# A hybrid decoder layer with mixture of experts: bias columns instead of bias products in the wide jobs, and folds moved to GpSimd

## The reference

```
hid = jnp.dot(xblk, w1[e]) + b1[e]            # 1024 -> 2048
glu = jnp.minimum(hid[:, 0::2], 7.0)
lin = jnp.clip(hid[:, 1::2], -7.0, 7.0)
act = glu * jax.nn.sigmoid(1.702 * glu) * (lin + 1.0)
yb  = jnp.dot(act, w2[e]) + b2[e]             # 1024 -> 1024, then times the gate
```

## Time and profile before

| | |
|---|---|
| median of three runs | 2207.58 us |
| the profiled execution | 2204.4 us |
| its span | 2202.7 us |
| TensorE (PE) busy | 2060.5 us, 94% |
| VectorE (DVE) busy | 1600.2 us, 73% |
| ScalarE (ACT) busy | 1294.2 us, 59% |
| GpSimd (POOL) busy | 420.0 us, 19% |
| mean granted TensorE clock | 0.973 |

### The profile page before, as it was taken

The page is one execution under the profiler, slowest core; times in us unless marked ns, Lnnn a source line. Parts: engine busy times, 40 slices in busy tenths (PEclk is TensorE's granted clock), DMA queues, the critical chain, the costliest instruction groups (busy, mean ns, idle before and its releaser), DMA issues. The chain is left out here.

```text
span 2202.7 us, 40551 instructions
## 1 busy us (share of the span) xinstructions
PE 2060.5 (94%) x11750; PEld 1774.1 (81%) x11751; DVE 1600.2 (73%) x2206; ACT 1294.2 (59%) x1867; POOL 420.0 (19%) x478
## 2 busy tenths in 40 slices
PE   7999978778967999999999999999999999999994
PEld 6888867777856888889798897889898888979883
DVE  5342166985657687978878787788788797887876
ACT  5221245563436576766757677677667676675765
POOL 3100000220231121211213122122212131121311
PEclk9999979999978999999999999999999999999997
DMA  5221120004346897979889798899798897988978
GB/s 182 61 82 54 43 96 1 11 20 140 106 163 241 284 314 242 353 250 329 290 269 332 240 351 267 296 313 358 254 318 299 259 348 250 332 284 276 332 240 309
DMA packets 260787, 506.10 MB, mean 230 GB/s; under 512 B 34369, under 2 KB 35394, under 8 KB 260440
## 3 DMA queue, kind: packets, MB, share of 16 engines
q1 hardware_dynamic: 242938, 458.05, 60.3%
q0 software_dynamic: 17792, 47.33, 8.8%
q10 hardware_dynamic: 4, 0.02, 0.0%
HBM read 466.10 MB, written 39.22 MB: 229 GB/s over the span
## 5 line engine op out<-in xcount | busy, mean ns | idle before, releaser
L1819 DVE TENSOR_TENSOR wlo<-raw,whi 128x1024 fp32r<-128x1024 f32 x774 | 931.3, 1218 | 72.2 <-ACT whi L1295 53.1
L1295 ACT ACTIVATE whi<-raw 128x1024 fp32r<-128x1024 f32 x775 | 845.3, 1116 | 216.4 <-PE ps L984 161.1
L982 PE MATMUL ps<-xT,whi 128*128 128x320 f32 x1920 | 524.8, 349 | 6.2 <-DMA brow<-brow_d 6.2
L984 PE MATMUL ps<-xT,wlo 128*128 128x160 f32 x1920 | 455.6, 237 | 0.0
L982 PEld LDWEIGHTS ps<-xT,whi 128*128 128x128 f32 x1920 | 363.5, 189 | 10.7 <-issue 6.0
L984 PEld LDWEIGHTS ps<-xT,wlo 128*128 128x128 f32 x1920 | 369.0, 192 | 0.2
L2087 POOL DMA_INDIRECT acc_d<-y,icur x64 | 102.7, 1604 | 943.2 <-ACT y L1329 880.6
L619 PE MATMUL ps<-whi,xT 128*128 128x512 f32 x544 | 215.8, 397 | 0.0
L619 PE MATMUL ps<-whi,aT 128*128 128x512 f32 x512 | 212.9, 416 | 1.3
L621 PE MATMUL ps<-whi,xT 128*128 128x512 f32 x544 | 213.0, 392 | 0.0
L620 PE MATMUL ps<-wlo,xT 128*128 128x512 f32 x544 | 212.8, 391 | 0.0
(11 more groups left out here) (299 smaller groups left out, 3540.4 us busy)
## 6 DMA issues: line engine op xcount, KB each, us to landing
raw<-in_w SPq DMA_DIRECT2D x780, 512.0 KB
raw<-in_w_in SPq DMA_DIRECT2D x16, 512.0 KB
xs<-in_x SPq DMA_DIRECT2D x8, 512.0 KB, 7.1
raw<-in_w_out SPq DMA_DIRECT2D x8, 512.0 KB
mix<-in_x SPq DMA_DIRECT2D x8, 512.0 KB, 4.1
acc_d<-mix SPq DMA_DIRECT2D x8, 512.0 KB
h_d<-h SPq DMA_DIRECT2D x8, 512.0 KB
mix<-acc_d SPq DMA_DIRECT2D x8, 512.0 KB, 7.7
```

The costliest lines, as they stand in the source:

```text
L982: pe.matmul(o2, wh[:, a, cols], xT2[:, :, k, 0:JOB_T], start=q == 0 and a == 0, stop=False, skip_group_check=True)
L984: m = pe.matmul(o, wl[:, a, cols], xT2[:, 0, k, 0:JOB_T], start=False, stop=q == QUARTERS - 1 and a == 1, skip_group_check=True)
L1295: act.activation(parted(slot(whis, s)), paired(raw_slot(s), s), ACT.Copy).then_inc(split_hi, 1)
L1819: dve.tensor_tensor(parted(slot(wlos, s)), paired(raw_slot(s), s), parted(slot(whis, s).bitcast(F32)), ALU.subtract).then_inc(split_lo, 1)
```

## The change

The b1 biases of the wide jobs leave TensorE's chains. In the front, TensorE transposes the raw biases of the 32 experts (gate and linear ones apart) into bank 1, VectorE copies them out (and adds 1 to the linear ones), SP writes them to DRAM and reads them back later, as columns, into a place that is free then. Before each job GpSimd copies the job's 2 x 8 columns into `bcur`. In a wide job ScalarE adds the gate bias as the activation's bias, in two activations instead of one, and VectorE adds the linear bias to `lsum` by one more operation. The fold of the 32 further rows is now done by GpSimd from SBUF: ScalarE evacuates both blocks (64 partitions) into `y`, GpSimd copies the lower block to `yfold` and adds it to the upper one. TensorE, ScalarE, VectorE, SP and GpSimd get the waits that go with it.

```diff
 # TensorE, between the halves of unit 0
+            def bias_turn():
+                pe.wait_ge(bias_in, 16 * 5)
+                pe.wait_ge(turned_lo, FIRST_FREE)
+                for two in range(2):
+                    for i in range(BTILES):
+                        cols = slice(2 * P * i + two, 2 * P * (i + 1) + two - 1, 2)
+                        m = pe.transpose(ps[:, 1, (two * BTILES + i) * NE:(two * BTILES + i + 1) * NE],
+                                         bp[0:NE, cols], ident[0:NE, 0:NE])
+                m.then_inc(bias_turned, 1)
+            bias_turn()
 # first_unit
+                if half == 1 and q == 0:
+                    pe.wait_ge(bturn_set, 1)
 # wide_step
-                        if q == 0:
-                            pe.matmul(o, brow[:, c * UNIT + 256 * odd + P * i:c * UNIT + 256 * odd + P * (i + 1)], ones2[:, 0:JOB_T],
-                                      start=False, stop=False, skip_group_check=True)
 # SP, before the wait for bias_hi; and before the router weights
+            sp.wait_ge(bturn_set, 1)
+            sp.dma_start(bcolT_d, bturn[:, :, :, :]).then_inc(bturn_out, 16)
...
+            sp.wait_ge(bturn_out, 16)
+            sp.dma_start(bcolT[:, :, :, :], bcolT_d).then_inc(bcolT_in, 16)
 # ScalarE: unit 0's chains; wide activation; block 1
+                        act.wait_ge(bturn_out, 16)
...
-                    act.activation(sigw[:, :, :], gsum[:, :, :], ACT.Gelu_apprx_sigmoid).then_inc(sig_set, 1)
+                    if c == 0:
+                        act.wait_ge(bcur_set, j + 1)
+                    for i in range(2):
+                        m = act.activation(sigw[:, i, :], gsum[:, i, :], ACT.Gelu_apprx_sigmoid,
+                                           bias=bcur[:, 0, 2 * c + i:2 * c + i + 1])
+                    m.then_inc(sig_set, 1)
...
-                    act.wait_ge(y_set[1], j * 2 + c - 3)
-                    act.activation(yfold[:, c - 4, :], ps[HALF:2 * HALF, out_bank(2, c, 1), :], ACT.Copy,
-                                   scale=gcur[HALF:2 * HALF, 1:2]).then_inc(yfolded, 1)
+                    act.activation(y[0:2 * HALF, 1, (c - 4) * UNIT:(c - 3) * UNIT], ps[0:2 * HALF, out_bank(2, c, 1), :], ACT.Copy,
+                                   scale=gcur[0:2 * HALF, 1:2]).then_inc(yfolded, 1)
 # VectorE: behind the lower bounds; the linear bias; y_fold and its calls are gone
+            dve.wait_ge(bias_turned, 1)
+            dve.tensor_copy(bturn[:, 0, :, :], ps[:, 1, 0:BTILES * NE].rearrange("p (i e) -> p i e", e=NE))
+            dve.tensor_scalar(bturn[:, 1, :, :], ps[:, 1, BTILES * NE:2 * BTILES * NE].rearrange("p (i e) -> p i e", e=NE),
+                              1.0, None, ALU.add).then_inc(bturn_set, 1)
...
+                dve.tensor_tensor(lsum[:, :, :], lsum[:, :, :],
+                                  bcur[:, 1, 2 * c:2 * c + 2].unsqueeze(2).broadcast_to([P, 2, JOB_T]),
+                                  ALU.add).then_inc(lin_biased, 1)
+                dve.wait_ge(lin_biased, j * 4 + c + 1)
 # GpSimd
+            def columns(e):
+                pool.tensor_copy(bcur[:, :, :], bcolT[:, :, :, e].rearrange("p a i o -> p a (i o)")).then_inc(bcur_set, 1)
+            def next_bias(j, e):
+                wait(act_set, j * 4 + 4)
+                columns(bass.ds(e, 1))
+                wait(bcur_set, j + 2)
+            def y_fold(j, c):
+                wait(yfolded, j * 2 + c - 3)
+                cols = slice((c - 4) * UNIT, (c - 3) * UNIT)
+                pool.tensor_copy(yfold[:, c - 4, :], y[HALF:2 * HALF, 1, cols]).then_inc(low_moved, 1)
+                pool.wait_ge(low_moved, j * 2 + c - 3)
+                pool.tensor_tensor(y[0:HALF, 1, cols], y[0:HALF, 1, cols], yfold[:, c - 4, :], ALU.add).then_inc(y_set[1], 1)
+                pool.wait_ge(y_set[1], j * 2 + c - 1)
 # GpSimd's job: behind load_slots; before the scatters
+                e = pool.value_load(jobt[0:1, 0, bass.ds(j + 1, 1)], min_val=0, max_val=NE - 1)
...
+                if blocks == 2:
+                    next_bias(j, e)
+                    y_fold(j, 4)
+                    y_fold(j, 5)
                 for b in ((0, 1) if blocks == 2 else (1, 0)):
+                    if b == 0 and blocks == 1:
+                        pool.sem_inc(low_moved, 2)
+                        next_bias(j, e)
```

More of the change, by code:

```diff
@@ L81 @@
 B_AV, B_HI, B_HG, B_OUT = 0, 128, 640, 1152
+BTILES = FF // P
 F32 = mybir.dt.float32
@@ L112, in build @@
     brow_d = dram("brow_d", (NE + 1, 2, BW))
+    bcolT_d = dram("bcolT_d", (P, 2, BTILES, NE))
     raw = at("raw", 0, [P, QUARTERS, 2, UNIT])
@@ L150, in build @@
     tinit = at("tinit", B + 68 * KB, [P, PAD_ROWS, 2])
+    bturn = at("bturn", B, [P, 2, BTILES, NE])
     hf = at("hf", B, [P, HH, T])
@@ L180, in build @@
     glw = at("glw", B + 55.75 * KB, [P, 2, 2, JOB_T])
+    bcur = at("bcur", B + 58.25 * KB, [P, 2, BTILES])
     yfold = at("yfold", B + 60 * KB, [HALF, 2, UNIT])
+    bcolT = at("bcolT", B + 64 * KB, [P, 2, BTILES, NE])
     R = [B + 72.5 * KB]
@@ L326, in build @@
         rooted, eps_set, brow_zero = sem("rooted"), sem("eps_set"), sem("brow_zero")
-        lin_set, yfolded = sem("lin_set"), sem("yfolded")
+        lin_set, yfolded, low_moved = sem("lin_set"), sem("yfolded"), sem("low_moved")
+        bias_turned, bturn_set, bturn_out, bcolT_in, bcur_set = (
+            sem(n) for n in ("bias_turned", "bturn_set", "bturn_out", "bcolT_in", "bcur_set"))
+        lin_biased = sem("lin_biased")
         pool_mark, sync_mark, act_mark = sem("pool_mark"), sem("sync_mark"), sem("act_mark")
@@ L342, in build @@
         FIRST = [0, 2, 4, 6, 1, 3, 5, 7]
+        FIRST_FREE = 2 * NT
         def x_bank(i):
@@ L1871, in hidden_wide @@
                 dve.wait_ge(sum_taken, j * 8 + 2 * c + 2)
+                if c == 0:
+                    dve.wait_ge(bcur_set, j + 1)
+                dve.tensor_tensor(lsum[:, :, :], lsum[:, :, :],
+                                  bcur[:, 1, 2 * c:2 * c + 2].unsqueeze(2).broadcast_to([P, 2, JOB_T]),
+                                  ALU.add).then_inc(lin_biased, 1)
+                dve.wait_ge(lin_biased, j * 4 + c + 1)
                 dve.tensor_scalar(lsum[:, :, :], lsum[:, :, :], 1.0 + LIMIT, 1.0 - LIMIT, ALU.min,
@@ L1886, in aT_wide @@
                                   aTh[:, k, 1, 0:HALF].bitcast(F32), ALU.subtract).then_inc(aT_lo, 1)
[L1888 to L1893, removed]
             def job(j, blocks):
@@ L1898, in job @@
                         (hidden if blocks == 1 else hidden_wide)(j, UNIT_END[s - 1])
-                    if blocks == 2 and UNIT_END.get(s - 1, 0) == 4:
-                        y_fold(j, 4)
                     jsplit(j, s + AHEAD)
@@ L1910, in job @@
                 if blocks == 2:
-                    y_fold(j, 5)
                     dve.sem_inc(hid_taken, 4)
@@ L1915, in job @@
                     dve.sem_inc(lin_set, 4)
+                    dve.sem_inc(lin_biased, 4)
             for s in range(4):
@@ L2106, in _ @@
             pool.wait_ge(y_zero, 1)
+            pool.wait_ge(bcolT_in, 16)
+            columns(slice(0, 1))
+            pool.wait_ge(bcur_set, 1)
             with pool.Fori(0, JOBS, 1) as j:
```

## The result

The kernel after has a median of 2219.29 us (2214.33 to 2229.77, nine runs), the kernel before 2209.54 us in the same nine rounds: ratio 1.0062, 95% interval 1.0049 to 1.0074, so slower, by some 14 us by the ratio. The profiled execution took 2224.26 us, with a span of 2222.6; the pair of profiles is 19.9 us apart, about twice the difference of the medians, and terms read from the pair have to be taken so.

A forecast was written before the change was run, and what follows sets the result against it. TensorE's instruction count was taken as the bound, with any transfer or engine late enough to stop it. 2204.4 - 29 + 16.5 + 22 - 2.4 = 2211.5, plus 3.2 for the median: 2215 us; 8-in-10 range 2195 to 2233.

The forecast's parts named there:

- Term 1: Wide jobs: 240 bias products leave TensorE's chains at 0.12 us each, a gain of 29 us.
- Term 2: Front: TensorE waits for VectorE's copies of the turned biases, 13.9 us plus 2.6 for half clock, a loss of 16.5 us.
- Rival 3: Front: VectorE copies before its small operations are through, TensorE hardly waits, some 1.5 us remain; 2200 us, chance 0.07.
- Term 3: Narrow jobs behind wide ones: GpSimd's folds delay scatters and gathers 3.4 us, TensorE stalls, a loss of 22 us.
- Term 4: Job stage: four of TensorE's waits for the bias row go as narrow jobs lengthen, a gain of 2.4 us.
- Rival 1: Narrow jobs: folds delay GpSimd under 1.3 us, gathers stay in time; 2193 us, up to 2203; chance 0.27.
- Rival 2: Nine tight narrow jobs, step 18: pauses of 2.5 us and more bring half clock, 2.6 us each; 2246 us, chance 0.11.
- Rival 4: Narrow jobs: GpSimd's locks starve VectorE and TensorE waits for splits, 1 us in each of 15; 2230 us, chance 0.05.

The follow-up runs named there:

- one memset: Changed kernel with folds back on ScalarE and VectorE, plus one GpSimd clear, waited for, ahead of a wide job's first scatter: 2205.34 us, ratio 0.9998 to the kernel before.

## Why the prediction was right, and where it was wrong

The sum came out: 2215 against 2219.29, slower as said, with 7 us of loss forecast and 14 measured by the ratio. Its steps did not all.

**Term 1, -29: right in kind, a little too large.** A wide job lasts 54.72 us instead of 56.54, 0.11 us for each bias product and 27 us in all. In the kernels without the wait for the row it is 55.0 (the 0.17 us wait for a bank is part of this): there the products are worth 15 x 1.53 = 23 us. The sentence "no product waits for the new additions" holds, but I did not look at what the shorter step runs into next.

**Term 2, +16.5: right.** Pause 12.85 us (49.70 to 62.55) where 13.9 was said, since GpSimd's third subtraction ended sooner than the old small operation suggested; half clock 2.6 us. The scores were 15.6 us late. Rival 3 had the right remedy: with the copies first TensorE hardly waits. The lockout is the rule of the Trainium skill (SBUF — State Buffer, "Who interferes with whom"). The trace agrees for the operations with two SBUF inputs (2.18 to 4.31 us for 4 elements). By the same section a VectorE instruction with at most one SBUF input, outside the modes that use both ports, doesn't contend with GpSimd. The trace agrees for the copies out of PSUM, which took 0.42 and 0.41 us beside GpSimd's subtraction; the operation at L1491, with one input and in SBUF, was held 2.39 us, and no run here shows in which mode it ran.

**Term 3, +22: the amount right, the mechanism wrong.** The folds cost 24 us (1.0114 alone; 1.0062 against 0.9955 in the change). GpSimd's delay was said to be 3.4 us and is 3.1; 1.30 us for the addition and 0.61 and 1.36 for the copies lie inside the bounds. What failed is "what is behind shifts alike. TensorE stalls" at the gathered rows. The first gather was issued only 1.7 us later, since the copy of the gates and the slots' transfer were shorter, and it landed about when it was wanted: 2.3 us of stalls instead of 20. The transfers themselves shifted, and they share 16 engines with the weights. The table by stretch, from the narrow job's start in steps of 2 us, before (last three columns: clock, share of the DMA engines, GB/s):

```profile
968.80:970.80 2.00, 2.00 (x10) 1.63 (x9) 1.29 (x3) 1.89 (x4) 0.06 (x1) 1.00 0.07 27
...
972.80:974.80 2.00, 2.00 (x11) 1.64 (x10) 2.00 (x2) 2.00 (x3) 1.44 (x2) 1.00 1.04 158
974.80:976.80 2.00, 2.00 (x10) 1.65 (x9) 2.00 (x3) 0.28 (x1) 1.44 (x2) 1.00 1.03 188
...
978.80:980.80 2.00, 2.00 (x10) 1.64 (x10) 1.98 (x3) 2.00 (x3) 0.57 (x2) 1.00 0.99 354
...
982.80:984.80 2.00, 2.00 (x12) 1.61 (x11) 1.98 (x4) 1.79 (x3) 0.00 (x0) 1.00 1.06 406
```

and after:

```profile
988.80:990.80 2.00, 2.00 (x11) 1.65 (x10) 1.22 (x2) 2.00 (x2) 1.92 (x2) 1.00 0.42 144
...
992.80:994.80 2.00, 2.00 (x10) 1.65 (x9) 2.00 (x4) 0.30 (x2) 1.70 (x2) 1.00 0.57 148
994.80:996.80 2.00, 2.00 (x10) 1.68 (x9) 1.96 (x3) 2.00 (x3) 1.39 (x3) 1.00 1.02 167
...
998.80:1000.80 2.00, 2.00 (x11) 1.64 (x10) 2.00 (x3) 1.21 (x3) 0.81 (x2) 1.00 1.04 276
```

Before, the scatter's traffic fills the engines from 4 to 8 us behind the start (158 to 188 GB/s), and from 10 us on the loads run at 354. After, the engines are mostly half busy until 8 us, and the scatter falls at 8 to 12 us, when loads have queued. The view of the transfers says whose traffic it is. From 972.8 to 976.8 us, before, GpSimd's queue has 0.57 MB and 94.3% of the engines, and SP's 0.13 MB and 9.5%. From 994.8 to 998.8 us, after, GpSimd's has 0.41 MB and 63.4%, and SP's 0.36 MB and 37.1%. In the first 16 us of the job GpSimd's queue moves 0.66 MB in both kernels and takes no more of the engines after (23.9% against 27.1%), but SP's moves 2.85 MB instead of 3.17. What is lost is the idle time ahead of the scatter. From there the engines are full to the end of the job (share 1.05), so the loads never make it up and the last of the queue, the row, has it all. These 0.32 MB are 0.8 us at 390 GB/s, and TensorE waits 1.82 us for this row; where the rest arises is not shown. I had read the row's wait as one that goes away. Its few waits were the sign that it had no margin: one memset, a scatter 1.1 us later, is enough for waits in ten of the fourteen other wide jobs.

**Term 4, -2.4: wrong in sign.** "The other four end narrow jobs that are now longer": the narrow jobs did not become longer at the gathers, so the row was not covered, and its waits grew by 17 us. I also missed that a wide job has no more use for this wait.

**The rivals.** Rival 1 (gathers in time) is nearly what happened, but not with its time, as another stall took the place. Rival 2 named the right mechanism, a dropped clock behind a stall, at the wrong place and with a pause of 2.5 us and more as its condition: five of the row's waits, of 1.70 to 1.89 us, cost 1.56 us each in this way. Rival 4's lock exists (28 us of longer splits) and costs little: without the row's wait the folds on GpSimd are worth 5 us in all.

**The sum.** In the pair of profiles it is -27.3 + 17.4 + 17.1 + 7.8 + 2.3 + 1.6 = +18.9 where the forecast had +7 and the spans differ by 19.9. The medians of the runs put the change at +9.8, the ratio at +14. So the forecast time stood partly by luck: a stall of 20 us that was not there, beside waits for the row and a lowered clock of 25 us that were not foreseen, a gain 2 us too large and a term of 2.4 us with the wrong sign. One profile of each kernel can't tell which of its stages is longer than in the median run.

## What to carry to other kernels

When an edit delays an engine that issues transfers, follow the bytes, not only the one transfer that engine waits for: the item last in a full queue is the one that became late here, small as it is (16 KB). A wait of a few tenths that shows up in a handful of jobs may say that there is no margin, and not that the transfer is cheap. And when an edit removes the use of a datum, remove the wait for it: here that one line was worth 25 us, as much as the products that the edit removed.

## What the runs showed of the hardware

- An indirect scatter with an add filled the 16 DMA engines (share 1.03 to 1.04, and 94.3% by GpSimd's queue alone) at 158 to 188 GB/s, where weight loads reached 406; moved some 3 us, with the same bytes, it cost 24 us.
- On GpSimd a 32x512 copy took 0.61 us with hardly a split of VectorE beside it and 1.36 beside one; the two-input addition took 1.29 to 1.30 in either place. A memset beside splits changed neither them nor itself (0.95 us).
- In the profile after, a stall of about 1.8 us was followed by half clock in five cases (1.70 to 1.89 us) and not in two others (1.87 and 1.83 us, before the wide jobs at 1628 and 1912); what decides between them is open.
